# Splitting the weights of a stage's last slab and the next two ahead of the norm, in buffers of their own

## The chip, the cores and the metric

The kernel runs on one core of one Trainium2 chip. The metric is the device time of one execution in microseconds (us), and the number given for a kernel is the median of its timed runs. TensorE (PE) multiplies, VectorE (DVE), ScalarE (ACT) and GpSimd (POOL) do the elementwise work, SyncE (SP) starts transfers. Each engine works through its own instructions in order and waits at semaphores for the others.

## The reference

Two layers of a decoder over x of 512 tokens by 1024 channels, all in float32. A layer runs three token mixers on the same x (a diagonal state-space model "S5", causal pooling, sparse attention), merges them with gates, multiplies by an output matrix, adds the residual and normalizes; then a SwiGLU feed-forward part does the same with its own output matrix and norm. Cut to what matters here:

```python
for l in range(2):
    m = merged(s5(u), pool(u), attention(q, k, v), gates)   # all of them products of x with w_in
    x = layer_norm(alpha * x + m @ w_out, g1, b1)            # norm 0 (layer 0), norm 2 (layer 1)
    h = silu(x @ w_gate) * (x @ w_up)
    x = layer_norm(alpha * x + h @ ffn_w_out, g2, b2)        # norm 1 (layer 0), norm 3 (layer 1)
```

Four norms, then: after three of them the next products need the new x, after the last (norm 3) the output is stored.

## The kernel before

**Products.** Every float32 factor is split in two rounded parts, high and low, and a product is three matmuls: high by high, low by high, high by low. The weights come as a stream of 264 slabs of 128 partitions by 1024 values. SP loads slab n into `raw[n % 2]` as soon as slab n-2 has been split; ACT writes its high part to `whi[n % 2]` (`split_hi`, L973), DVE its low part to `wlo[n % 2]` (`split_lo`, L1373), PE multiplies. ACT's split of slab n waits until PE has finished slab n-2, whose buffer it overwrites: `slab_done` counts finished slabs from 2 up, so "slab n-2 done" is the value n+1.

**An output stage** (`to_tokens`, L587) makes 4 token tiles of 128 by 1024 in PSUM: the first 512 channels with the stage's first half of slabs, the other 512 with the second. Its last slab, b, uses the ordinary buffer `b % 2`. Token tile 3 is finished last, behind the first turning back.

**A norm** works on two halves of the tokens (tiles 0 and 1, tiles 2 and 3). For a half DVE takes statistics from PSUM (L1443), ACT the root (L986), DVE the scalars (L1457, L1459); the normalized tile goes to `xt` by DVE (`first_columns`, L1480, the first 512 channels) and by ACT (`normalized`, L988, the rest); PE turns it back to channels by tokens with 16 transposes (`turn_back`, L575); ACT applies gain and shift in four quarters of 256 channels (`gained`, L997, which raises `ln_x`); DVE splits each quarter into `xh` and `xl` (`halves`, L1461, which raises `x_ready`).

**The first pair of slabs after a norm** (`first_pair`, L616; slabs "at" and "at+1") can start before all of x is there. `x_quarter` (L543) is 6 matmuls of one slab, one token half and one quarter of the channels. In the kernel before the order is: slab at with the first token half, all 4 quarters; `turn_back` of the second half; slab at+1 with the first half; slab at with the second half, at which it counts as done; slab at+1 with the second half. The splits of these two slabs stand in the middle of the norm on ACT (L1015, L1020) and on DVE (L1494, L1509).

**What follows the pair** is slab at+2, in `x_slab` (L537). Its split needs `whi[0]`, and its wait, written once for all slabs, is for slab at done. ACT has one more step ahead of it which waits for the same: it reads slab at's result from PSUM (the tanh in L1357 in the feed-forward part, the copy in L1051 at the start of a layer).

**GpSimd at the start of layer 1** (from L456): it waits for the end of layer 0's last stage, starts two transfers of 2 MB (`w1`, weights of the attention's compression) to SBUF; waits for the whole of the new x and stores it to DRAM in four transfers (`scr_x`); then computes the powers of the state-space model, which it ends with `lam_ready` and, much later, `eph_ready`. DVE waits for the first in `coefficients`, for the second in its first `scan` (L1687). Ahead of each of its waits POOL drains, and it makes the descriptors of its own transfers.

Of the kernel before, what the change touches and what calls it, by code (L numbers as in the profile page):

```python
# [72 lines left out]
def build_program(nc, wstream, w1s, smalls, norms, consts, xin, pos, out):  # L73
# [45 lines left out]
    gates = place("gates", big_at, [P, 16, S])  # L119
    xt = place("xt", xf_at, [P, 4, D])  # L120
# [134 lines left out]
    with ctx:  # L255
# [155 lines left out]
        def _(pool):  # L411
# [44 lines left out]
            for l in range(L):  # L456
# [69 lines left out]
        def _(pe):  # L526
# [16 lines left out]
            def x_quarter(n, half, g, x_before):  # L543
# [4 lines left out]
                for k in (2 * g, 2 * g + 1):  # L548
                    wh, wl = whi[:, n % 2, k * P:k * P + P], wlo[:, n % 2, k * P:k * P + P]
# [14 lines left out]
            def token_products(slot, fh, t, k0, hi, lo, last):  # L564

                dst = ps[:, tile_bank(fh, t), :]
                for q in range(2):
                    a, b = hi[:, k0 + q, P * t:P * t + P], lo[:, k0 + q, P * t:P * t + P]
                    wh, wl = whi[:, slot, S * q:S * q + S], wlo[:, slot, S * q:S * q + S]
# [5 lines left out]
            def turn_back(n, half, rt):  # L575

                if half == 0 or n == 2 * L - 1:
                    pe.wait_ge(ln_first, n + half + 1)
# [8 lines left out]
            def to_tokens(n, at, pairs, hi, lo, freed, taken, each, rt):  # L587

                for fh in range(2):
# [3 lines left out]
                    for s in range(pairs - 2 * fh):  # L593
# [4 lines left out]
                        for t in range(4):  # L598
                            m = token_products(c % 2, fh, t, 2 * s, hi, lo, fh == 0 and s == pairs - 1)
                        m.then_inc(slab_done, 1)  # L600
                a, b = at + 2 * pairs - 2, at + 2 * pairs - 1
                k = 2 * pairs - 4
                pe.wait_ge(lo_ready, a + 3)
                for t in (0, 1):
                    token_products(a % 2, 1, t, k, hi, lo, False)
                pe.wait_ge(lo_ready, b + 3)
                for t in (0, 1):
                    token_products(b % 2, 1, t, k + 2, hi, lo, True).then_inc(t_psum, 1)
                for t in (2, 3):
                    m = token_products(a % 2, 1, t, k, hi, lo, False)  # L610
                m.then_inc(slab_done, 1)
                token_products(b % 2, 1, 2, k + 2, hi, lo, True).then_inc(t_psum, 1)
                turn_back(n, 0, rt)
                token_products(b % 2, 1, 3, k + 2, hi, lo, True).then_inc(slab_done, 1)

            def first_pair(n, at, rt):  # L616

                pe.wait_ge(lo_ready, at + 3)
                for g in range(4):
                    x_quarter(at, 0, g, n * 8)  # L620
                if n:
                    turn_back(n - 1, 1, rt)
                pe.wait_ge(lo_ready, at + 4)
                for g in range(4):
                    x_quarter(at + 1, 0, g, n * 8)
                for c in range(2):
                    for g in range(4):
# [1520 lines left out]
```

## Time and profile before

| what | value |
|---|---|
| time, median of 3 runs | 1764.71 us (1764.57 to 1766.1) |
| the profiled execution, first to last instruction | 1767.2 us |
| PE busy | 1733.0 us, 98% of the span |
| DVE busy | 944.0 us, 53% |
| ACT busy | 649.2 us, 37% |
| POOL busy | 125.6 us, 7% |
| mean clock granted to TensorE | 0.997 of full speed |
| share of PE in the chain that ended last | 86% |

The profile is one execution, which took 2.5 us more than the median of the timed runs. PE is busy nearly everywhere, so what matters are the few places at which it waits, or runs at the lower of its two clocks; the means of the page don't show these. In the rows below a line of the timeline has the start in us, the duration in us, the engine, the line of the kernel, the operation, out<-in, partitions by elements, the count, and in brackets how long the engine had been idle and for whom.

### The profile page before, as it was taken

The page shows a single profiled execution, that of the slowest core. Times are in us where ns is not written, and L with a number is a line of the kernel's source. Part 1 is how long each engine was busy: PE and PEld are TensorE (multiplying, and loading weights), DVE is VectorE, ACT ScalarE, POOL GpSimd, SP SyncE. Part 2 cuts the span into 40 slices and gives each one's busy share as a digit, 9 for nine tenths or more (in the row PEclk, how much of TensorE's full clock was granted, in tenths as well). Part 3 has the DMA queues.
Part 4 walks back from the last instruction along what each step waited for, and adds up shares of the span by engine and source line. Part 5 has one row for each costly group of instructions (what it writes and reads, how often), then busy time and mean ns, then how long its engine had stood idle before and what let it go on. Part 6 is the DMA issues. An engine that isn't in the chain of part 4 may idle for free.

```text
span 1767.2 us, 26801 instructions
## 1 busy us (share of the span) xinstructions
PE 1733.0 (98%) x10172; PEld 1409.5 (80%) x10172; DVE 944.0 (53%) x1514; ACT 649.2 (37%) x1152; POOL 125.6 (7%) x252
## 2 busy tenths in 40 slices
PE   7999999999999999999999999999999999999998
PEld 6778777788888888888888777777888888888886
DVE  5788778444354444422358877775453544444223
ACT  4333666422252222221353346664222522222112
POOL 4700000000000000000037000000000000000000
PEclk9999999999999999999999999999999999999999
DMA  7443111133513222222263431112233222222222
GB/s 259 157 117 88 53 50 49 49 101 102 169 63 105 95 95 95 95 96 95 91 244 110 116 86 50 53 37 72 96 119 119 82 98 95 95 95 95 96 96 83
DMA packets 65918, 174.88 MB, mean 99 GB/s; under 512 B 14256, under 2 KB 26576, under 8 KB 65056
## 3 DMA queue, kind: packets, MB, share of 16 engines
q1 hardware_dynamic: 40192, 140.53, 24.5%
q10 hardware_dynamic: 21888, 13.64, 3.2%
q0 software_dynamic: 3744, 19.41, 3.2%
q8 instruction: 66, 1.08, 0.3%
q14 instruction: 28, 0.23, 0.1%
HBM read 162.27 MB, written 7.08 MB: 96 GB/s over the span
## 4 chain that ended last, share of the span: by engine, by line
PE 86%; DVE 7%; DVEq 3%; ACT 2%; issue 1%; DMA 0%; ACTq 0%
PE ps L532 19%; PE ps L534 18%; PE ps L533 18%; PE ps L572 6%; PE ps L570 6%; PE ps L571 6%; PE ps L857 2%; PE ps L844 2%; PE ps L830 1%; DVE wlo L1376 1%; PE ps L550 1%; PE ps L561 1%; PE ps L552 1%; PE ps L551 1%; PE ps L583 1%
## 5 line engine op out<-in xcount | busy, mean ns | idle before, releaser
L532 PE MATMUL ps<-xh,whi 128*128 128x512 f32 x1312 | 520.0, 396 | 8.4 <-ACT gates L1190 5.1
L534 PE MATMUL ps<-xh,wlo 128*128 128x512 f32 x1312 | 511.3, 390 | 0.0
L533 PE MATMUL ps<-xl,whi 128*128 128x512 f32 x1312 | 510.9, 389 | 0.0
L1376 DVE TENSOR_TENSOR wlo<-raw,whi 128x1024 fp32r<-128x1024 f32 x264 | 324.9, 1231 | 347.4 <-ACT whi L977 338.2
L977 ACT ACTIVATE whi<-raw 128x1024 fp32r<-128x1024 f32 x264 | 278.9, 1057 | 351.0 <-PE ps L572 234.3
L532 PEld LDWEIGHTS ps<-xh,whi 128*128 128x128 f32 x1312 | 246.4, 188 | 61.4 <-issue 7.8
L534 PEld LDWEIGHTS ps<-xh,wlo 128*128 128x128 f32 x1312 | 246.3, 188 | 52.3
L533 PEld LDWEIGHTS ps<-xl,whi 128*128 128x128 f32 x1312 | 246.6, 188 | 48.8 <-issue 0.5
L570 PE MATMUL ps<-whi,hh 128*128 128x512 f32 x352 | 137.5, 391 | 0.0
L572 PE MATMUL ps<-whi,hl 128*128 128x512 f32 x352 | 137.0, 389 | 0.0
L571 PE MATMUL ps<-wlo,hh 128*128 128x512 f32 x352 | 137.0, 389 | 0.0
L1360 ACT ACTIVATE hh<-fb 128x512 f32 (+1 forms) x44 | 27.8, 632 | 201.8 <-DVE fb L1382 201.8
L1382 DVE TENSOR_TENSOR fb<-fa,ps 128x512 f32<-128x512 f32 x44 | 30.2, 687 | 110.9 <-PE ps L534 110.7
L416 POOL TENSOR_TENSOR carry<-carry 1x1 f32<-1x1 f32 x21 | 5.2, 248 | 1176.2 <-PE ps L572 419.5
L1977 DVE SCALAR_TENSOR_TENSOR fa<-ft,ps 128x512 f32<-128x512 f32 x44 | 30.3, 688 | 99.5 <-ACT ft L1357 99.5
L572 PEld LDWEIGHTS ps<-whi,hl 128*128 128x128 f32 x352 | 66.1, 188 | 13.8
L570 PEld LDWEIGHTS ps<-whi,hh 128*128 128x128 f32 x352 | 66.1, 188 | 13.7 <-DVE wlo L1376 0.3
L571 PEld LDWEIGHTS ps<-wlo,hh 128*128 128x128 f32 x352 | 66.1, 188 | 13.6
L1357 ACT ACTIVATE ft<-ps 128x512 f32<-128x512 f32 x44 | 26.3, 598 | 132.7 <-PE ps L534 128.7
L1255 ACT ACTIVATE prob<-ps,tiny 128x128 f32<-128x128 f32 (+3 forms) x128 | 66.3, 525 | 20.4 <-DVE tiny L1802 20.3
L1802 DVE TENSOR_REDUCE tiny<-ps 128x2 f32<-128x256 f32 (+3 forms) x64 | 52.4, 819 | 11.8 <-PE ps L833 11.8
L550 PE MATMUL ps<-xh,whi 128*128 128x256 f32 x128 | 39.5, 309 | 15.7 <-DVE wlo L1376 9.9
(338 smaller groups left out, 2335.5 us busy)
## 6 DMA issues: line engine op xcount, KB each, us to landing
raw<-wstream SPq DMA_DIRECT2D x264, 512.0 KB, 3.3
w<-w1s POOLq DMA_DIRECT2D x4, 2048.0 KB, 11.7
sm<-smalls POOLq DMA_DIRECT2D x2, 1060.0 KB, 6.7
xt<-xin ACTq DMA_DIRECT2D x4, 512.0 KB, 6.3
scratch_u<-pa ACTq DMA_DIRECT2D x8, 256.0 KB
toep<-scratch_k ACTq DMA_DIRECT2D x4, 512.0 KB
toep_b<-scratch_k ACTq DMA_DIRECT2D x4, 512.0 KB
xt<-xin POOLq DMA_DIRECT2D x4, 512.0 KB, 4.0
```

Of the source, the lines that this page charges most:

```text
L532: pe.matmul(ps[:, bank, :], wh, hi[:, k, :], start=first and i == 0, stop=False)
L533: pe.matmul(ps[:, bank, :], wh, lo[:, k, :], start=False, stop=False)
L534: m = pe.matmul(ps[:, bank, :], wl, hi[:, k, :], start=False, stop=last and i == len(blocks) - 1)
L550: pe.matmul(dst, wh, xh[:, k, cols], start=k == 0, stop=False)
L570: pe.matmul(dst, a, wh, start=False, stop=False)
L571: pe.matmul(dst, a, wl, start=False, stop=False)
L572: m = pe.matmul(dst, b, wh, start=False, stop=last and q == 1)
L844: m = pe.transpose(ps[:, bank, at + P * k:at + P * k + P], prob[:, i % 3, kv, P * k:P * k + P], ident)
L977: act.activation(whi[:, c % 2, :], raw[:, c % 2, :], ACT.Copy).then_inc(hi_ready, 1)
L1255: x = act.activation(prob[:, i % 3, kv, 0:n], ps[:, sbank(i) + kv, 0:n], ACT.Exp, bias=tiny[:, 28 + 8 * (i % 3) + kv:29 + 8 * (i % 3) + kv ...
L1376: dve.tensor_tensor(wlo[:, c % 2, :], raw[:, c % 2, :], whi[:, c % 2, :].bitcast(f32), SUB).then_inc(lo_ready, 1)
L1802: dve.tensor_reduce(tiny[:, 28 + 8 * (i % 3):30 + 8 * (i % 3)], ps[:, sbank(i):sbank(i) + 2, 0:n], AX.X, MAX, negate=True).then_inc(s_max, 1)
```

## The change

The last slab b of each output stage and, before norms 0 to 2, the two slabs at and at+1 are split into new buffers, `whi_end` and `wlo_end`, three slots each. These lie where `hh` or `gates` lie, whose first blocks nobody reads any more by then. The splits of all three now wait for slab b-3 done and stand ahead of the norm on ACT and on DVE (`stage_splits`, `split_end_hi`, `split_end_lo`); no split is left in the norm.

`first_pair` takes its quarters in turn through both slabs: quarters 0 and 1 of at, 0 and 1 of at+1, then 2 and 3 alternately; then the turning back; then each quarter of the second token half for at and for at+1. Slab at therefore counts as done 6 matmuls ahead of slab at+1, where before it was 24. The very first pair of the kernel keeps its old order (`first_slabs`). The split of slab at+2 and its wait are unchanged.

In the norm DVE takes the second quarter ahead of the last tile's statistics, and the normalized first 512 channels of tile 3 stay with DVE while those of tile 2 stay with ACT, so that ACT has three such steps instead of four. POOL stores x first, then waits for slab at+1 done (since `w1` lies over the new buffers) and then loads `w1`. The diff, cut:

```diff
+    whi_end = place("whi_end", big_at, [P, 3, 1024], f32r)
+    wlo_end = place("wlo_end", big_at + 3072, [P, 3, 1024], f32r)
...
                 if l:
-                    wait(slab_done, l * NSLAB + 2)
-                    load_w1()
-
-                if l:
                     wait(ln_x, l * 16)
                     for t in range(4):
                         pool.dma_start(scr_x[:, t, :], xt[:, t, :]).then_inc(x_stored, 16)
+                    wait(slab_done, l * NSLAB + 4)
+                    load_w1()
...
             def first_pair(n, at, rt):
 
+                pe.wait_ge(lo_ready, at + 4)
+                for c, g in ((0, 0), (0, 1), (1, 0), (1, 1), (0, 2), (1, 2), (0, 3), (1, 3)):
+                    x_quarter(at + c, 0, g, n * 8)
+                turn_back(n - 1, 1, rt)
+                for g in range(4):
+                    for c in range(2):
                         m = x_quarter(at + c, 1, g, n * 8)
-                    m.then_inc(slab_done, 1)
+                        if g == 3:
+                            m.then_inc(slab_done, 1)
...
+            def split_end_hi(c, slot, free):
+
+                act.wait_ge(raw_loaded[c % 2], (c // 2 + 1) * 16)
+                act.wait_ge(slab_done, free + 3)
+                act.activation(whi_end[:, slot, :], raw[:, c % 2, :], ACT.Copy).then_inc(hi_ready, 1)
+
+            def stage_splits(at, pairs, last):
+
+                b = at + 2 * pairs - 1
+                split_end_hi(b, 0, b - 3)
+                if not last:
+                    split_end_hi(b + 1, 1, b - 3)
+                    split_end_hi(b + 2, 2, b - 3)
...
-                    for fh in (0, 1) if half and n < 2 * L - 1 else (1,):
+                    for fh in (0, 1) if t == 2 and n < 2 * L - 1 else (1,):
...
                 first_columns(0)
                 second_stats(n, 2, next_slab + 2)
-                if not last:
-                    split_lo(0, next_slab)
                 halves(n, 0, 0, rt, last)
-                if last:
-                    halves(n, 0, 1, rt, last)
+                halves(n, 0, 1, rt, last)
                 second_stats(n, 3, next_slab + 2)
                 variances(1)
...
-                    halves(n, 0, 1, rt, last)
+                    halves(n, 0, 2, rt, last)
                     scalars(n, 1)
-                    for g in (2, 3):
-                        halves(n, 0, g, rt, last)
-                    split_lo(0, next_slab + 1)
+                    halves(n, 0, 3, rt, last)
+                    first_columns(1)
```

What stands in a row on DVE in norm 0 of the kernel before, from the statistics of tile 2 to the end of the first token half (`wlo` is a split of weights, CAST and the TENSOR_TENSOR to `xl` are one quarter of x):

```order
L1443 BN_STATS lnst<-ps 128x6 [waits t_psum]
L1445 BN_AGGR lnmv<-lnst 128x2
L1376 TENSOR_TENSOR wlo<-raw,whi 128x1024 [waits hi_ready]
L1474 CAST xh<-xt 128x2x256 [waits ln_x]
L1382 TENSOR_TENSOR xl<-xt,xh 128x2x256
L1443 BN_STATS lnst<-ps 128x6 [waits slab_done]
L1445 BN_AGGR lnmv<-lnst 128x2
L1451 TENSOR_SCALAR lnrs<-lnmv 128x2
L1474 CAST xh<-xt 128x2x256 [waits ln_x]
L1382 TENSOR_TENSOR xl<-xt,xh 128x2x256
L1457 RECIPROCAL lnrs<-lnrs 128x2 [waits ln_sd]
L1459 SCALAR_TENSOR_TENSOR lnnb<-lnmv,lnrs 128x2
```

And of the changed kernel, from the same statistics on (`L1477` and `L1479` are the statistics there):

```order
L1477 BN_STATS lnst<-ps 128x6 [waits t_psum]
L1479 BN_AGGR lnmv<-lnst 128x2
L1508 CAST xh<-xt 128x2x256 [waits ln_x]
L1416 TENSOR_TENSOR xl<-xt,xh 128x2x256
L1508 CAST xh<-xt 128x2x256 [waits ln_x]
L1416 TENSOR_TENSOR xl<-xt,xh 128x2x256
L1477 BN_STATS lnst<-ps 128x6 [waits slab_done]
L1479 BN_AGGR lnmv<-lnst 128x2
L1485 TENSOR_SCALAR lnrs<-lnmv 128x2
L1508 CAST xh<-xt 128x2x256 [waits ln_x]
L1416 TENSOR_TENSOR xl<-xt,xh 128x2x256
L1491 RECIPROCAL lnrs<-lnrs 128x2 [waits ln_sd]
```

The split of the weights is gone from this stretch and the second quarter has moved ahead of the last tile's statistics.

On POOL at the start of layer 1, before (`w` is `w1`, the memsets of `php` begin the powers):

```order
L416 TENSOR_TENSOR carry<-carry 1x1 [waits slab_done]
L465 DMA w_58<-w1s 128x4096 x2
L416 TENSOR_TENSOR carry<-carry 1x1 [waits ln_x]
L474 DMA scratch_x<-xt 128x1024 x4
L416 TENSOR_TENSOR carry<-carry 1x1 [waits sincos_ready]
L477 MEMSET php 128x16
```

And of the changed kernel:

```order
L418 TENSOR_TENSOR carry<-carry 1x1 [waits ln_x]
L472 DMA scratch_x<-xt 128x1024 x4
L418 TENSOR_TENSOR carry<-carry 1x1 [waits slab_done]
L467 DMA w_60<-w1s 128x4096 x2
L418 TENSOR_TENSOR carry<-carry 1x1 [waits sincos_ready]
L477 MEMSET php 128x16
```

The store of x and the load of `w1` have changed places, and the wait between them is now for finished slabs.

## Rows read from the trace of the kernel before

**Rows 1.** Timeline of PE, norm 0: turning back, last tile, first pair.
```profile
507.90 0.49 PE L583 MATMUL ps<-cn,xt 128*128 128x128 f32 x3
...
510.80 0.40 PE L572 MATMUL ps<-whi,mgl 128*128 128x512 f32 x1
511.75 0.36 PE L550 MATMUL ps<-xh,whi 128*128 128x256 f32 x1 [0.56 <-DVE xl L1382]
...
513.89 0.39 PE L550 MATMUL ps<-xh,whi 128*128 128x256 f32 x1 [1.19 <-DVE xl L1382]
...
517.86 0.49 PE L583 MATMUL ps<-cn,xt 128*128 128x128 f32 x3
519.52 0.36 PE L550 MATMUL ps<-xh,whi 128*128 128x256 f32 x1
```

**Rows 2.** Timeline of DVE and ACT in norm 0.
```profile
508.54 3.75 ACT L1006 ACTIVATE xt<-ps,nrm 128x256 f32<-128x256 f32 x8 [0.20 <-PE ps L583]
...
509.27 1.23 DVE L1376 TENSOR_TENSOR wlo<-raw,whi 128x1024 fp32r<-128x1024 f32 x1 [0.19 <-issue]
...
510.91 0.69 DVE L1382 TENSOR_TENSOR xl<-xt,xh 128x512 fp32r<-128x512 f32 x1
...
513.14 0.69 DVE L1382 TENSOR_TENSOR xl<-xt,xh 128x512 fp32r<-128x512 f32 x1
...
514.18 2.78 ACT L993 ACTIVATE xt<-ps,lnnb,lnrs 128x512 f32<-128x512 f32 x4 [0.26 <-DVE lnnb L1459]
...
514.55 0.69 DVE L1382 TENSOR_TENSOR xl<-xt,xh 128x512 fp32r<-128x512 f32 x1
...
520.04 0.69 DVE L1382 TENSOR_TENSOR xl<-xt,xh 128x512 fp32r<-128x512 f32 x1
...
521.15 0.69 DVE L1382 TENSOR_TENSOR xl<-xt,xh 128x512 fp32r<-128x512 f32 x1
```

**Rows 3.** Windows: length, busy (instructions) of PE, PEld, DVE, ACT, POOL; clock, DMA, GB/s.
```profile
96.00:97.00 1.00, 1.00 (x5) 0.81 (x6) 1.00 (x2) 0.00 (x0) 0.00 (x0) 1.00 0.52 76
515.00:516.00 1.00, 1.00 (x5) 0.70 (x5) 0.93 (x3) 1.00 (x2) 0.00 (x0) 0.50 0.00 0
```

**Rows 4.** Timeline behind the first pair after norm 0, four engines.
```profile
525.24 0.28 PE L552 MATMUL ps<-xh,wlo 128*128 128x256 f32 x1
...
525.56 0.60 ACT L1357 ACTIVATE ft<-ps 128x512 f32<-128x512 f32 x1 [2.02 <-PE ps L552]
...
527.13 1.22 DVE L1376 TENSOR_TENSOR wlo<-raw,whi 128x1024 fp32r<-128x1024 f32 x1 [0.26 <-ACT whi L977]
...
528.41 0.50 PE L532 MATMUL ps<-xh,whi 128*128 128x512 f32 x1
```

**Rows 5.** Timeline of PE: the same two ends at norms 1 and 2.
```profile
878.96 0.49 PE L583 MATMUL ps<-cn,xt 128*128 128x128 f32 x3
...
899.75 0.50 PE L532 MATMUL ps<-xh,whi 128*128 128x512 f32 x1
...
1383.00 1.58 PE L583 MATMUL ps<-cn,xt 128*128 128x128 f32 x13
...
1402.59 0.50 PE L532 MATMUL ps<-xh,whi 128*128 128x512 f32 x1
```

**Rows 6.** Timeline of PE in layer 0: the longest wait inside the stages.
```profile
95.90 0.50 PE L532 MATMUL ps<-xh,whi 128*128 128x512 f32 x1 [1.95 <-DVE wlo L1376]
```

**Rows 7.** Timeline of POOL, PE and DVE at the start of layer 1.
```profile
882.46 0.57 POOL L465 DMA_DIRECT2D w<-w1s  x1
...
910.75 0.18 POOL L416 TENSOR_TENSOR carry<-carry 1x1 f32<-1x1 f32 x1 [8.90 <-issue]
...
964.96 0.13 POOL L506 MEMSET r8m<- 128x16 f32 x1
...
970.59 0.50 PE L532 MATMUL ps<-xh,whi 128*128 128x512 f32 x1 [0.75 <-DVE wlo L1376]
...
977.28 0.42 DVE L1382 TENSOR_TENSOR sct<-eph,ps 128x256 f32<-128x256 f32 x1 [0.16 <-issue]
```

More of the change, by code:

```diff
@@ L562, in residual, with token_products @@
                                   start=m == 0, stop=False, is_transpose=True)
-            def token_products(slot, fh, t, k0, hi, lo, last):
+            def token_products(high, low, fh, t, k0, hi, lo, last):
                 dst = ps[:, tile_bank(fh, t), :]
@@ L1018, in ln_part @@
                 deviations(n, 1)
-                if not last:
-                    split_hi(0, next_slab + 1)
                 normalized(n, 1, rt)
@@ L1344, in _ @@
                         merged_hi(c // 5 - 1)
-                for c in range(1, NO):
+                for c in range(1, NO - 1):
                     split_hi(0, l * NSLAB + OO + c)
@@ L1348, in _ @@
                         merged_hi(3)
+                stage_splits(l * NSLAB + OO, KD // 2, False)
                 ln_part(l * 2, l * NSLAB + OF, xt)
@@ L1365, in _ @@
                     ff_pairs(hl_ + OF // 2 + 2 + i * 2, i + 1, False)
-                for c in range(1, NG):
+                for c in range(1, NG - 1):
                     split_hi(0, l * NSLAB + OG + c)
+                stage_splits(l * NSLAB + OG, KF // 2, l == L - 1)
                 ln_part(l * 2 + 1, (l + 1) * NSLAB, xt)
@@ L1480, in first_columns @@
                 def first_columns(half):
-                    for t in (2 * half, 2 * half + 1):
+                    for t in (2 * half, 2 * half + 1) if half == 0 or last else (3,):
                         x = dve.tensor_scalar(rt[:, t, 0:S], ps[:, tile_bank(0, t), :], lnmv[:, t, 0:1], lnrs[:, t:t + 1], SUB, MUL)
@@ L1492, in ln_part @@
                 second_stats(n, 2, next_slab + 2)
-                if not last:
-                    split_lo(0, next_slab)
                 halves(n, 0, 0, rt, last)
-                if last:
-                    halves(n, 0, 1, rt, last)
+                halves(n, 0, 1, rt, last)
                 second_stats(n, 3, next_slab + 2)
@@ L1957, in _, with stage @@
                         x.then_inc(mg_raw, 1)
-                def stage(at, pairs, last_low=False):
-                    for c in range(1, 2 * pairs):
+                def stage(at, pairs, last_low=False, last=False):
+                    b = at + 2 * pairs - 1
+                    for c in range(1, 2 * pairs - 1):
                         if c == pairs + 1:
@@ L1965, in stage @@
                             low_parts(3)
+                    split_end_lo(b, 0)
+                    if not last:
+                        split_end_lo(b + 1, 1)
+                        split_end_lo(b + 2, 2)
                 stage(l * NSLAB + OO, KD // 2, True)
@@ L1991, in _ @@
                     ff_pairs(hl_ + OF // 2 + 2 + i * 2, i + 1, False)
-                stage(l * NSLAB + OG, KF // 2)
+                stage(l * NSLAB + OG, KF // 2, last=l == L - 1)
                 ln_part(l * 2 + 1, (l + 1) * NSLAB, xt)
```

48 lines of the change are left out of this document (29 added, 19 removed).

## The prediction

> **What bounds the kernel now.** I read the page first: PE is busy 98% of the span, so only its waits and its slow stretches can be gained. The waits of PE send me to the three norms that are followed by products, and the timeline of PE there gives the shape. I count from t0, the first transpose of the first turning back (507.90 in norm 0). PE starts its last matmul of token tile 3 at 510.80, is free 0.23 us later, at t0+3.1, waits 0.56 us for the first quarter of x and 1.19 us for the second [rows 1]. The reason is DVE: a split of weights of 1.23 us at 509.27 stands ahead of the first quarter, whose low part only starts at 510.91, and the statistics of tile 3 stand between it and the second quarter, which starts at 513.14 [rows 2]. The windows show a second loss: in 515 to 516 PE is busy all the time, but at a granted clock of 0.50, the lower level of 1.2 GHz [rows 3]. At the other end, slab at+2 starts at 528.41 [rows 4], t0+20.5. The same stretch takes 899.75 - 878.96 = 20.8 us at norm 1 and 1402.59 - 1383.00 = 19.6 us at norm 2 [rows 5]. I take 19.6 us as its length at full clock, and the 0.9 and 1.2 us more as the price of the slow clock in norms 0 and 1.
>
> **The change, part by part.**
>
> *The first token half.* ACT starts the gains at t0+0.64 and needs 3.75 / 4 = 0.94 us for a quarter [rows 2]. Without the split, DVE starts when the first quarter lands. The second token half shows how long that is: turning back starts at 517.86 [rows 1], the low part of its first quarter starts at 520.04 and takes 0.69 [rows 2], 2.87 us in all. So the first quarter is there at t0+2.9, before PE is free at t0+3.1: the wait of 0.56 goes. The second quarter follows 1.1 us later (520.04 to 521.15), at t0+4.0. The third stands behind the statistics; the distance 510.91 to 513.14, 2.2 us, puts it at t0+6.2. The fourth comes 1.4 us behind it (513.14 to 514.55, scalars included), at t0+7.6 [rows 2]. PE: a quarter of one slab is 6 matmuls; between the first behind the turning back at 519.52 [rows 1] and the last of slab at at 525.24 [rows 4] lie 47 steps, 0.122 us each, so 0.73 us for a quarter. It takes quarter 0 of at (to 3.9), then quarter 1 and both of at+1 (4.0 to 6.2), both third quarters (to 7.7), both fourth (to 9.2). All four waits are covered by the other slab. The second turning back needs ACT as well: three steps of the four that take 2.78 [rows 2], 2.1 us, from about t0+6.6, is t0+8.7, earlier. It starts at t0+9.2.
>
> *The second token half.* In the kernel before, slab at+1's first half, 24 matmuls, stood behind this turning back and covered the 2.87 us until the next quarter of x. Now nothing stands there. The transposes take 519.52 - 517.86 = 1.66 us [rows 1], to t0+10.9; the quarter is there at t0+12.1: a new wait of 1.2 us. From there PE needs 1.46 us for a quarter of both slabs and DVE delivers one every 1.1, so 48 matmuls run through, to t0+17.9. So far the change is ahead by 1.5 us: in norm 2 the pair ended 0.2 us before slab at+2 started, at 19.4.
>
> *What is late next: the split of slab at+2.* ACT must wait for slab at done, read its result from PSUM, then split; DVE then makes the low part. In the kernel before: last matmul of at 525.24, ACT 525.56, DVE 527.13 for 1.22, PE 528.41, 3.17 us, hidden behind the 24 matmuls of at+1 [rows 4]. The queue is the same in the changed kernel, but at is now done only 6 matmuls ahead of at+1. The last matmul of at starts at 12.1 + 41 x 0.122 = t0+17.1; plus 3.17 is t0+20.2. PE is free at t0+17.9 and waits 2.3 us. On ACT the reading and the split stand behind that wait, DVE's split behind ACT, everything of slab at+2 behind both. At norm 1 the copy of L1051 takes the place of the tanh, with the same length.
>
> *Sum of a norm at full clock:* 20.2 against 19.6, so 0.6 us worse, three times: +1.8 us. Against what the profiled execution took (20.5, 20.8, 19.6) it is 60.6 - 60.9 = -0.3 us.
>
> *The clock.* In norm 0 the waits of 0.56 and 1.19 us brought the slow clock [rows 1, 3]; by the lengths norm 1 had it too and norm 2 had not; in layer 0 one wait of 1.95 us [rows 6] did not bring it either, 96 to 97 ran at 1.00 [rows 3]. The changed norm has 1.2 us and, 6 us later, 2.3 us in one piece, longer than any of those. I give each norm a chance of 0.65. The price is bounded below by what it cost before, 0.9 us, where part of it hid behind waits for x, and above by a stretch like 514 to 517.6, 3.6 us at half speed, 1.8 us; behind the pair PE has no waits for tens of us, so I take the upper end. Two of three: +3.6 us.
>
> *The splits ahead of the norm.* The same number of instructions, moved to before the first statistics, where ACT and DVE wait for PE. No gain and no loss: PE's matmuls of slab b followed without a gap before. If the loads came late, DVE's 1.23 us splits would push the statistics; I bound that at 0 to 0.7 us a norm and take 0. Norm 3 and the first pair of the kernel keep their order: 0.
>
> *POOL in layer 1.* Its store and its load, issue and descriptors together, took from 882.46 to 910.75, 28.3 us, a good part of it before x was whole [rows 7]. Now both lie behind it. The last gain of norm 1 ends at 878.96 + 9.2 + 0.6 + 3.75 = 892.5, so the powers begin near 920 to 921 instead of 911, 9 to 10 us later, and `eph_ready` moves from 965 to about 974.5. DVE reads these values at 977.28 [rows 7]: still in time, by under 3 us. A gain is possible too: in 943 to 970 DVE worked beside POOL's largest instructions and PE waited 0.75 us at the end of it [rows 7]; with POOL later that can vanish, no more. Bounds -0.75 and +4, taken: -0.3, near the lower one because the margin holds.
>
> As to this, the Trainium skill (GPSIMD Engine Reference, section 8, Key points) says that GpSimd shares its SBUF interfaces with VectorE and contends with DVE instructions of two SBUF inputs. DVE's part of this stretch is mostly such instructions; by that rule the contention moves with POOL and the sum would stay within the same bounds.
>
> **Sum.** The profiled execution: 1767.2 - 0.3 + 3.6 - 0.3 = 1770.2. It lies 2.5 us over the median of the timed runs, about what its two slow stretches cost (0.9 + 1.2), so I take the typical timed run to have full clock in the norms: 1764.7 + 1.8 + 3.6 - 0.3 = 1769.8; allowing for a slow stretch in some runs of before, 1769.5.
>
> **The rivals.** A measurement can tell about 0.2%, 3.5 us, from no change; so faster is under 1761.2 and slower over 1768.2.
>
> 1. *The clock holds or falls once.* Everything as above, but the gap leaves the clock mostly alone: 1764.7 + 1.5 = 1766.2, or 1768 with one. For it: norm 2 and the wait of 1.95. Against it: norms 0 and 1 fell with less in one piece. Chance 0.30. The Trainium skill (TensorE: Matmul & The Clock Gate, HAM oscillation) would have only idle gaps clearly longer than these re-throttle the array; by that rule this rival is the outcome, but this trace shows the lower level after gaps of 0.56 and 1.19 us, so the rows decide against giving it more.
>
> 2. *The handover does not cost* because the reading and the split overlap with the end of at+1 more than I see, or the second half runs ahead: then the pair's gain stands, 17.9 + 0.2 against 19.6, -1.5 x 3 = -4.5, and with -0.3 it is 1760. Nothing in the rows shortens the 3.17 us. Chance 0.05.
>
> 3. *POOL comes too late.* If descriptors or contention stretch its chain by more than 3 us, DVE's scan waits, and PE, which needs the scan's result some 6 us later, waits with it: +1 to +4 on top, 1773. Chance 0.10, from a drift of 3 in a chain of 55 us.
>
> 4. *All three norms fall:* 1771.3. Chance 0.15. The forecast with two has 0.40.
>
> **How the numbers follow.** The predicted time is that of the forecast, 1769.5. Slower: forecast 0.40, all three 0.15, POOL 0.08 of its 0.10, makes 0.63. Same: the first rival 0.30 and 0.02 of the third, 0.32. Faster: 0.05. The range takes in the clock holding everywhere with the small bounds below it (1765.5) and POOL's case (1773.5).
>
> **What would show it.** In the profile of the changed kernel: no wait for x of over 0.3 us in the first token half; the second turning back at t0+9.2; then PE waiting 1.2 us for `xl`; then 2.3 us at the first matmul of slab at+2 with the split of the weights on DVE as releaser, three times; half clock in the first us of that slab. On POOL the powers near 920, DVE's scan without a wait. I am wrong if slab at+2 starts within 0.5 us of the pair's end, if the turning back comes later than t0+10, or if PE waits anew between 970 and 990.

## The result and the profile after

The changed kernel takes 1774.46 us (median of 4 runs, 1771.99 to 1775.45), the kernel before 1764.64 us in the same comparison. The ratio is 1.0048, 95% interval [1.0035, 1.006]: slower, by some 8.5 us. A second comparison, below, gives 1.0036 [1.0022, 1.0049]. The profiled execution of the changed kernel has a span of 1772.0 us from first to last instruction and took 1773.82, so the rows below are those of a typical run.

In every run that has both numbers the time is 1.7 to 1.9 us longer than the span. The 1767.2 us of the profile before are a span, so that execution took some 1769 us. It lay about 4.3 us over the median and not 2.5, which matters for the prediction's view of the clock.

The waits of PE, summed over the whole profile of the changed kernel, name the places at once (columns: total us, times, longest):

```profile
PE ps L532 <- DVE wlo L1405: 11.7, 6, 3.0
...
PE ps L553 <- DVE xl L1416: 3.1, 3, 1.0
```

The first row is the first matmul of a slab waiting for the low part of its weights; the second is the first quarter of x behind the second turning back. In norm 0 the timeline of PE in the changed kernel reads as follows (start, length, line, operands, and in brackets the idle time before and what ended it); [rows 1, 4] are what it answers to.

```profile
507.48 1.91 PE L585 MATMUL ps<-cn,xt 128*128 128x128 f32 x16
...
516.71 1.91 PE L585 MATMUL ps<-cn,xt 128*128 128x128 f32 x16
519.64 0.39 PE L553 MATMUL ps<-xh,whi_end 128*128 128x256 f32 x1 [1.03 <-DVE xl L1416]
...
527.84 0.50 PE L532 MATMUL ps<-xh,whi 128*128 128x512 f32 x1 [2.18 <-DVE wlo L1405]
```

Between 510.4 and 516.7 nothing stands idle any more: the waits of 0.56 and 1.19 us of [rows 1] are gone. In their place stand 1.03 and 2.18 us. ACT and DVE show why the second one is there (same kernel, same place):

```profile
524.98 0.60 ACT L1385 ACTIVATE ft<-ps 128x512 f32<-128x512 f32 x1 [2.58 <-PE ps L555]
525.48 1.05 ACT L994 ACTIVATE whi<-raw 128x1024 fp32r<-128x1024 f32 x1
...
526.56 1.23 DVE L1405 TENSOR_TENSOR wlo<-raw,whi 128x1024 fp32r<-128x1024 f32 x1 [0.26 <-ACT whi L994]
```

ACT waits 2.58 us for slab at, reads its result, makes the high part, DVE makes the low part, and only then can slab at+2 begin. It is the same chain as in [rows 4], but the matmuls of slab at+1 no longer stand behind it. At the other two norms the same two starts read:

```profile
880.50 1.94 PE L585 MATMUL ps<-cn,xt 128*128 128x128 f32 x16 [0.38 <-ACT xt L1024]
...
900.91 0.50 PE L532 MATMUL ps<-xh,whi 128*128 128x512 f32 x1 [2.17 <-DVE wlo L1405]
...
1387.08 1.91 PE L585 MATMUL ps<-cn,xt 128*128 128x128 f32 x16
...
1407.45 0.50 PE L532 MATMUL ps<-xh,whi 128*128 128x512 f32 x1 [2.17 <-DVE wlo L1405]
```

The clock behind the wait of 2.2 us, in windows of 1 us behind norm 0, norm 1 and norm 2 (columns as in [rows 3]; the third number from the end is the granted clock):

```profile
530.00:531.00 1.00, 1.00 (x4) 0.80 (x3) 0.85 (x2) 0.18 (x1) 0.00 (x0) 0.50 0.62 246
902.00:903.00 1.00, 1.00 (x4) 0.75 (x3) 0.30 (x2) 1.00 (x1) 0.56 (x2) 0.50 0.97 328
...
1408.00:1409.00 1.00, 1.00 (x6) 0.80 (x5) 0.30 (x2) 0.79 (x2) 0.00 (x0) 1.00 0.51 115
```

It fell to the level of 1.2 GHz behind norms 0 and 1 and stayed at 2.4 GHz behind norm 2.

The largest single loss lies elsewhere, in layer 1 (timeline of PE; before it was 0.75 us at 970.59 [rows 7]):

```profile
975.59 0.50 PE L532 MATMUL ps<-xh,whi 128*128 128x512 f32 x1 [2.98 <-DVE wlo L1405]
```

The windows behind that wait show the lower clock once more:

```profile
977.00:978.00 1.00, 1.00 (x4) 0.81 (x3) 0.85 (x3) 0.00 (x0) 0.00 (x0) 0.50 1.18 220
```

DVE ahead of it, in the changed kernel, and POOL beside it:

```profile
962.10 0.43 DVE L1416 TENSOR_TENSOR hgt<-hid 128x256 f32<-128x256 f32 x1
...
964.44 1.37 DVE L1416 TENSOR_TENSOR ta<-lam,bch 128x512 f32<-128x512 f32 x1
965.73 1.53 DVE L1416 TENSOR_TENSOR tb<-lam,bch 128x512 f32<-128x512 f32 x1
...
971.96 1.60 DVE L1416 TENSOR_TENSOR vmat_b<-ta,tb 128x512 f32<-128x512 f32 x1
973.49 2.05 DVE L1405 TENSOR_TENSOR wlo<-raw,whi 128x1024 fp32r<-128x1024 f32 x1
```

```profile
964.22 2.50 POOL L444 TENSOR_TENSOR r8m<-eph,st 128x512 f32<-128x512 f32 x2
...
971.48 1.54 POOL L444 TENSOR_TENSOR eph<-r8m 128x512 f32<-128x512 f32 x1
973.14 1.31 POOL L504 COPY r8m<-rp 128x1024 f32<-128x1024 f32 x1
974.58 0.12 POOL L506 MEMSET r8m<- 128x16 f32 x1
```

and the same DVE instructions in the kernel before, where POOL's last large step had ended at 964.96 [rows 7]:

```profile
965.21 0.69 DVE L1382 TENSOR_TENSOR ta<-lam,bch 128x512 f32<-128x512 f32 x1
...
968.71 0.69 DVE L1382 TENSOR_TENSOR vmat_b<-ta,tb 128x512 f32<-128x512 f32 x1
969.32 1.22 DVE L1376 TENSOR_TENSOR wlo<-raw,whi 128x1024 fp32r<-128x1024 f32 x1
```

Six instructions of 0.69 us took 1.37 to 1.63 us each beside POOL's, and the split behind them 2.05 instead of 1.22. From the first of them to the end of the split it is 11.1 us instead of 5.3, so 5.8 us more. DVE had come to them 3.5 us earlier in the stage (its start moved from 965.21 to 964.44, while PE's program stood 2.8 us later by then), so 2.2 us of it came out as idle time of PE, and the slow stretch came on top.

To add up, I use the first transpose of each first turning back, t0, as a milestone. It cuts the program into three stretches: A from norm 0 to norm 1, B from norm 1 to norm 2 with the stages of layer 1, C from norm 2 to norm 3. C holds one norm and no POOL work, and in most kernels no slow stretch either. "Falls" counts the slow stretches of the clock behind norms 0, 1 and 2; the one in 977 to 978 is not among them and lies in B.

| profiled execution | A | B | C | falls |
|---|---|---|---|---|
| before | 371.06 | 504.04 | 370.13 | 2 |
| changed | 373.02 | 506.58 | 370.88 | 2 |
| changed, second profile | 372.82 | 506.55 | 370.86 | 2 |

Changed against before is +2.0, +2.5 and +0.75 us; t0 of norm 0 itself came 0.4 us earlier, so the span is 4.8 us longer. The medians differ by more (9.8 us in the first comparison, 6.8 in the second). The profiled execution of before is one with two slow stretches, as the prediction said.

### The profile page after: what moved, and what is told of

Same layout as the page of the kernel before. It is cut to its first block, busy times and chain, and to the rows that moved or that the text cites. A ratio compares the mean times of both kernels' runs of the same rounds, so it can differ in the third digit from the quotient of the medians.

```text
span 1772.0 us, 26801 instructions
## 1 busy us (share of the span) xinstructions
PE 1735.2 (98%) x10172; PEld 1413.0 (80%) x10172; DVE 944.8 (53%) x1517; ACT 647.1 (37%) x1149; POOL 125.6 (7%) x252
## 3 DMA queue, kind: packets, MB, share of 16 engines
q8 instruction: 66, 1.08, 0.3%
## 4 chain that ended last, share of the span: by engine, by line
PE 87%; DVE 6%; ACT 3%; DVEq 2%; issue 1%; DMA 1%; ACTq 0%; SPq 0%
PE ps L532 19%; PE ps L534 18%; PE ps L533 18%; PE ps L573 6%; PE ps L574 6%; PE ps L575 6%; PE ps L874 2%; PE ps L861 2%; PE ps L847 1%; PE ps L553 1%; DVE wlo L1405 1%; PE ps L554 1%; PE ps L555 1%; PE ps L690 1%; PE ps L564 1%
## 5 line engine op out<-in xcount | busy, mean ns | idle before, releaser
L1405 DVE TENSOR_TENSOR wlo<-raw,whi 128x1024 fp32r<-128x1024 f32 x254 | 312.9, 1232 | 336.2 <-ACT whi L994 327.2
L994 ACT ACTIVATE whi<-raw 128x1024 fp32r<-128x1024 f32 x254 | 268.4, 1057 | 333.3 <-PE ps L575 216.7
L573 PE MATMUL ps<-whi,hh 128*128 128x512 f32 x336 | 131.2, 391 | 0.0
L575 PE MATMUL ps<-whi,hl 128*128 128x512 f32 x336 | 130.9, 390 | 0.0
L574 PE MATMUL ps<-wlo,hh 128*128 128x512 f32 x336 | 130.9, 390 | 0.0
L874 PEld LDWEIGHTS ps<-probt,vtok 128*64 128x64 f32 x640 | 33.6, 136 | 23.0 <-issue 23.0
```

The lines of the kernel that those rows point to most:

```text
L573: pe.matmul(dst, a, wh, start=False, stop=False)
L574: pe.matmul(dst, a, wl, start=False, stop=False)
L575: m = pe.matmul(dst, b, wh, start=False, stop=last and q == 1)
L874: pe.matmul(ps[64 * kv:64 * kv + 64, 7, P * t:P * t + P], vtok[:, br, k, 64 * kv:64 * kv + 64], probt[:, i % 2, kv, P * k:P * k + P], star ...
L994: act.activation(whi[:, c % 2, :], raw[:, c % 2, :], ACT.Copy).then_inc(hi_ready, 1)
L1405: dve.tensor_tensor(wlo[:, c % 2, :], raw[:, c % 2, :], whi[:, c % 2, :].bitcast(f32), SUB).then_inc(lo_ready, 1)
```

## The experiments

The theory after the comparison: three things move the time. The quarters remove waits (gain), slab at+2 waits for the handover (loss), and POOL's exchanged order puts its large steps beside DVE instructions that PE is waiting for (loss). Rivals: the exchanged order costs because its results or `w1` come too late; or the 3 us wait is an accident of one execution. Kernels that are compared in one table below shared their runs of before.

**POOL's order taken back, all else changed.** The two end slabs of norm 1 move into buffers of their own, so that `w1` can be loaded where it was.

```diff
+    whi_alt = place("whi_alt", ys_at, [P, 2, 1024], f32r)
+    wlo_alt = place("wlo_alt", ys_at + 2048, [P, 2, 1024], f32r)
...
                 if l:
+                    wait(slab_done, l * NSLAB + 2)
+                    load_w1()
                     wait(ln_x, l * 16)
                     for t in range(4):
                         pool.dma_start(scr_x[:, t, :], xt[:, t, :]).then_inc(x_stored, 16)
-                    wait(slab_done, l * NSLAB + 4)
-                    load_w1()
```

> The changed kernel with one part undone: POOL again loads w1 first and stores x behind it, as in the kernel before (to allow it, the two slabs after norm 1 are split into a place that w1 does not cover). Theory A (POOL's later chain of powers works beside DVE's longest instructions and delays the split that PE waits for near 975 us): that wait falls from 2.98 us back to under 1 us, no slow clock follows it, and the kernel is 3 to 4 us faster than the changed one, about 6 us (0.34%) slower than the kernel before. Rival B (all of the loss is the handover at the norms): no change against the changed kernel, ratio 1.005, and a wait of about 3 us stays near 975 us.

**POOL's order alone, in the kernel before.** The same four lines the other way round, nothing else.

> The kernel before with only POOL's order changed: x is stored first, w1 loaded after slab at+1. Theory A: the powers start 9 us later, PE waits about 3 us instead of 0.75 near 971 us, a stretch at the lower clock may follow; 2 to 4 us slower than the kernel before (0.11 to 0.23%). Rival B: within 1 us of the kernel before.

**Alternating alone, in the kernel before.**

```diff
-                for c in range(2):
-                    for g in range(4):
-                        m = x_quarter(at + c, 1, g, n * 8)
-                    m.then_inc(slab_done, 1)
+                for i in range(8):
+                    c, g = (i % 2, i // 2) if n else (i // 4, i % 4)
+                    m = x_quarter(at + c, 1, g, n * 8)
+                    if g == 3:
+                        m.then_inc(slab_done, 1)
```

> The kernel before with only one thing changed: behind norms 0 to 2 the second token half of the first pair goes quarter by quarter through both slabs, so that slab at is done 6 matmuls ahead of slab at+1 instead of 24. Theory H (the split of slab at+2 waits for slab at done): PE waits 2.2 us behind each of the three pairs, in some followed by the lower clock (1.8 us each); slower by 6.6 to 12 us (0.37 to 0.68%). Rival (the handover's chain overlaps with the pair and costs little): within 2 us of the kernel before.

**The handover taken away from the changed kernel.** ACT and DVE split slab at+2 right behind the norm, when the last quarter of x has been made, and not after slab at.

```diff
+            def split_next_hi(at):
+                act.wait_ge(raw_loaded[0], (at // 2 + 2) * 16)
+                act.wait_ge(slab_done, at + 1)
+                act.activation(whi[:, 0, :], raw[:, 0, :], ACT.Copy).then_inc(hi_ready, 1)
...
+                split_next_hi(l * NSLAB + OF)
...
+                split_lo(0, l * NSLAB + OF + 2)
```

> The changed kernel with one addition: slab at+2 is split right behind the norm on ACT and DVE, without waiting for slab at done, since its buffer is free by then. Theory H: the waits of 2.2 us behind the three pairs vanish and with them the lower clock there; the kernel gains 6.6 us and 1.8 us for each slow stretch of the changed one, 8 to 11 us, and ends within 2 us of the kernel before, with the loss near 975 us left. Rival (the lower clock comes from the wait of 1.0 us behind the second turning back, or from elsewhere): slow stretches stay and the gain is 6 us at most.

Measured, all four beside the same 22 runs of before (median 1767.66 us):

| kernel | median us | ratio | A | B | C | falls |
|---|---|---|---|---|---|---|
| changed, POOL as before | 1769.76 | 1.0014 [1.0005, 1.0023] | 371.15 | 503.15 | 370.89 | 1 |
| before, POOL exchanged | 1773.20 | 1.0031 [1.0018, 1.0043] | 371.75 | 506.61 | 370.13 | 1 |
| before, alternating | 1776.01 | 1.0045 [1.0031, 1.0059] | 374.13 | 504.38 | 375.02 | 5 |
| changed, early split | 1769.69 | 1.0007 [0.9998, 1.0016] | 368.72 | 510.24 | 368.41 | 0 |

POOL's order is a cost of its own. Added to the kernel before it makes 5.5 us; taken out of the changed one, stretch B falls from 506.55 to 503.15, by 3.4 us, while C stays at 370.9, and no wait of over 0.3 us is left near 975. Two expectations were off in size. The changed kernel with POOL as before was to stay about 6 us over the kernel before and stays 2.1 over it; the early split was to gain 8 to 11 us on the changed kernel and gains 5 to 7 by the ratios. In the kernel with the exchanged order alone PE stands still for the same reason as in the changed one, at the next split in the row (first fence PE, second DVE):

```profile
980.49 0.76 PE L530 MATMUL ps<-xh,whi 128*128 128x512 f32 x1 [4.22 <-issue]
```

```profile
973.69 1.45 DVE L1380 TENSOR_TENSOR ta<-lam,sm 128x576 f32<-128x576 f32 x1
...
976.74 1.67 DVE L1393 SCALAR_TENSOR_TENSOR wmat_b<-ta,tb 128x576 f32<-128x576 f32 x1
978.33 2.05 DVE L1374 TENSOR_TENSOR wlo<-raw,whi 128x1024 fp32r<-128x1024 f32 x1
```

The profile puts this wait down to "issue", but the split on DVE ends at 978.33 + 2.05 = 980.38 and PE starts 0.11 us later. So when the profile names no releaser, it is worth a look at the other engines.

The alternation alone shows the handover in its pure form: it adds a wait of 2.18 us ahead of slab at+2 to the waits that the kernel before has anyway (PE, norm 2):

```profile
1392.80 0.39 PE L550 MATMUL ps<-xh,whi 128*128 128x256 f32 x1 [1.24 <-DVE xl L1383]
1394.21 0.58 PE L550 MATMUL ps<-xh,whi 128*128 128x256 f32 x1 [0.44 <-DVE xl L1383]
1409.96 0.50 PE L532 MATMUL ps<-xh,whi 128*128 128x512 f32 x1 [2.18 <-DVE wlo L1377]
```

Here the clock fell twice at norm 1 and twice at norm 2, and once behind norm 0. C is 4.9 us longer than in before. With the early split instead, A and C are the shortest of the table, 368.4 for C against 370.88 of the changed kernel: 2.5 us a norm, the 2.2 us of the handover and a little more. Its B is the longest, though (510.24): two waits of 2.68 and 4.22 us stand there, at 929.33 and 979.91, with POOL's order still the exchanged one. The second is the contention again. The first is not: the DVE instructions ahead of it take 0.68 to 0.78 us. There ACT's split was late, since its slab had not landed (ACT, early split):

```profile
917.62 1.06 ACT L994 ACTIVATE whi<-raw 128x1024 fp32r<-128x1024 f32 x1 [5.72 <-DMA raw<-wstream]
```

POOL issued `w1`, 4 MB, at 899.70 here, 18 us ahead of that split; in the kernels with POOL's order of before it is issued near 882 to 884. That the load held the slab back is likely, but not shown by itself. If both waits are the work of POOL's order, they must go with it; the next group tests that.

**Contention or lateness?** The kernel before, with POOL kept busy beside DVE and with nothing moved:

```diff
                 pool.memset(r8m[:, :, 0:1], 0.0).then_inc(eph_ready, 1)
+                if l:
+                    for i in range(6):
+                        tt(spare[:, :], sin_t[:, 0:448], cos_t[:, 0:448], MUL)
+                        pool.drain()
```

> The kernel before, with six more POOL products of 128x448 f32 (each followed by a drain, into 448 elements of free space, from the two rotation tables) right behind the memset of r8m that releases eph_ready in layer 1. POOL's powers, its loads and every wait stand where they stood, so nothing of POOL's comes later that anyone needs before 980 us; what is new is only that POOL works from about 965.1 to 974 beside DVE. Theory 1 (contention: DVE's operations with two SBUF inputs take about twice as long beside POOL's): the six 512-element operations of DVE at 965.2 to 969.3 take 1.4 to 1.6 us each, not 0.69, and the low split behind them 2.0, not 1.22, so the split that PE waits for at 970.59 comes 4 to 5 us later, PE stands idle 4 to 6 us in place of 0.75, the granted clock falls to 0.5 for some 3 us behind it, and the time rises by 5 to 8 us, as with the order of POOL alone (+5.5). Theory 2 (lateness: the exchanged order costs because w1, the powers or eph_ready come later): DVE's rows unchanged, time within 1 us of before.

**Slab by slab instead of alternating**, in the changed kernel with POOL's order of before:

```diff
-                for g in range(4):
-                    for c in range(2):
-                        m = x_quarter(at + c, 1, g, n * 8)
-                        if g == 3:
-                            m.then_inc(slab_done, 1)
+                for c in range(2):
+                    for g in range(4):
+                        m = x_quarter(at + c, 1, g, n * 8)
+                    m.then_inc(slab_done, 1)
```

> The changed kernel with POOL's order of before, and with the second token half slab by slab (four quarters of slab at, then four of at+1) in place of alternating. Nothing is left out of the computation. With the alternation this kernel took 1769.76 us beside 1767.66 of before (+2.1). Theory 1 (the alternation's handover costs: the split of slab at+2 waits for slab at, 6 matmuls ahead in place of 24): the 2.17 us idle piece at slab at+2 goes at norms 1 to 3; in its place each quarter of slab at waits about 0.4 us for its xl (DVE hands over a quarter each 1.1 us, PE uses it in 0.7), some 1.0 to 1.3 us per norm, so some 1 us per norm and the clock's fall are saved: 1766 to 1768, -2 to -4 us against the alternating one. Theory 2 (alternating hides as much as it costs): within 1 us of 1769.8.

**Both costs taken out**: early split and POOL's order of before, together in the changed kernel.

> The changed kernel with both suspected costs taken out: slab at+2 is split right behind the norm, without waiting for slab at (so the 2.2 us handover cannot arise), and POOL loads w1 ahead of its powers, as in the kernel before (the two next slabs of norm 1 then lie in buffers at ys_at, outside w1). Nothing is left out of the computation. Theory (handover and POOL's place are the two costs, the rest of the change gains): the kernel with early splits alone stood at +2.0 us against before (1769.69 to 1767.66) and the order of POOL alone at +5.5 (1773.2 to 1767.66), so 2.0 - 5.5 = -3.5 us: about 1764, ratio 0.998; no PE idle piece over 0.3 us at slab at+2 of any norm, none near 976 to 981, only the 1.0 us wait for xl behind the second turning back; granted clock full behind the norms. Rival (the gains of the quarters are worth nothing, the early splits only move the cost): within 0.1% of before, 1766 to 1769.

**The changed kernel again**, beside the same runs of before:

> The changed kernel itself, for its ratio on the same chip as the other three and a second profile. From the first measurement 1.0048 [1.0035, 1.006]; with before near 1767.7 on this chip some 1776. If POOL's place (+5.5 alone, -6.3 when taken back) and the handover explain it: idle pieces of 2.2 us at slab at+2 of the three norms and of about 3 us near 975.6, the latter in every profile. Rival (the 3 us piece belongs to one execution): gone here.

Measured, beside 19 runs of before (median 1766.79 us):

| kernel | median us | ratio | A | B | C | falls |
|---|---|---|---|---|---|---|
| before, POOL busy | 1773.02 | 1.0031 [1.0021, 1.0041] | 371.57 | 507.97 | 370.13 | 2 |
| changed, POOL as before, slab by slab | 1765.75 | 0.9992 [0.9983, 1.0001] | 370.31 | 503.33 | 369.88 | 0 |
| changed, early split, POOL as before | 1760.10 | 0.9960 [0.9946, 0.9974] | 368.93 | 499.32 | 368.40 | 0 |
| changed | 1773.60 | 1.0036 [1.0022, 1.0049] | 372.82 | 506.55 | 370.86 | 2 |

For the wait near 976 it is contention, not lateness: six products that nobody waits for cost 6.2 us by the medians, with the same ratio of 1.0031 as the exchanged order, and stretch B alone is 3.9 us longer. Its rows differ from what I had expected in the place: POOL was done with its powers at 962, so the products ran from there. POOL, then DVE, then PE:

```profile
962.02 8.70 POOL L443 TENSOR_TENSOR spare<-sin_t,cos_t 128x448 f32<-128x448 f32 x6
```

```profile
962.38 2.15 DVE L1381 TENSOR_TENSOR wlo<-raw,whi 128x1024 fp32r<-128x1024 f32 x1
964.45 1.37 DVE L1387 TENSOR_TENSOR hgt<-hid 128x256 f32<-128x256 f32 x1
965.90 1.08 DVE L1721 TENSOR_SCALAR hgt<-hgt 128x256 f32<-128x256 f32 x1
...
969.81 1.47 DVE L1387 TENSOR_TENSOR ta<-lam,bch 128x512 f32<-128x512 f32 x1
971.20 0.68 DVE L1387 TENSOR_TENSOR tb<-lam,bch 128x512 f32<-128x512 f32 x1
```

```profile
975.97 0.51 PE L537 MATMUL ps<-xh,whi 128*128 128x512 f32 x1 [3.84 <-DVE wlo L1381]
```

The same instruction `hgt<-hid` takes 0.43 us in the changed kernel at 962.10, where POOL was at small steps, and 1.37 here. With POOL's last product over at 970.72, DVE is back at 0.68 us for 512 elements. Of the six steps that were expected to suffer only the first did (1.47 us), but those ahead of them did, and the end is the same: the split that PE needs is late. PE also waits 1.14 us at 964.63, 0.1 us behind the end of the split of 2.15 us.

Slab by slab gives back 3.9 us against the alternating kernel (ratios 1.0014 and 0.9992, 0.22% of 1767), and 1.0 us of stretch C, as the first theory had it: the idle piece ahead of slab at+2 is gone at every norm, the clock did not fall, and the waits of the quarters that take its place are all under 0.3 us each. With both costs out the two waits of 2.68 and 4.22 us are gone (0.34 us is left at 966.96), B is 499.32, and the kernel beats before: 1760.10 us, 0.9960. That is more than the 0.998 that was expected from adding the two effects. They don't simply add: with the early split the exchanged order costs 10.9 us of B (510.24 against 499.32), with the handover in place 3.4. The two waits make 6.9 us of the first, and the clock is low beside them, in 930 to 934 and in 978 to 985.

**One quarter behind the second turning back.** In the fastest version the wait for `xl` of 1.03 us is left. One quarter moves behind the turning back to cover it, and the fastest version runs again beside it.

```diff
-                for c, g in ((0, 0), (0, 1), (1, 0), (1, 1), (0, 2), (1, 2), (0, 3), (1, 3)):
+                for c, g in ((0, 0), (0, 1), (1, 0), (1, 1), (0, 2), (1, 2), (0, 3)):
                     x_quarter(at + c, 0, g, n * 8)
                 turn_back(n - 1, 1, rt)
+                x_quarter(at + 1, 0, 3, n * 8)
```

> The fastest version so far (early splits, POOL's order of before; 1760.1 us beside 1766.79 of before on its chip), with one quarter of the first token half moved behind the second turning back, to cover its 1.03 us wait for xl. The turning back then starts some 0.5 us earlier (it waits some 0.2 us for the normalized values), and a quarter takes 0.7: of the 1.03 us some 0.5 stay. Theory (what PE waits for there sets the time): 0.5 us less at each of three norms, 1.5 in all, so 0.9950 to 0.9955 of before, beside 0.996. Rival (ACT's and DVE's chain behind the second turning back sets the end of the pair, so that order on PE matters only where it moves that start): the wait behind it shrinks by 0.7 but 0.2 to 0.5 comes back ahead of the turning back, under 0.5 us in all, not to be told from 0.996.

> The fastest version so far once more, as the thing to compare the moved quarter with on the same chip, and to see whether its ratio to before, 0.996 [0.9946, 0.9974] on the other chip, stands. Theory (POOL's place and the handover were the two costs, the quarters gain): again 0.995 to 0.997. Rival (the 3 us beyond the 3.5 that were expected there belonged to that chip): 0.998.

Measured beside 10 runs of before (median 1766.56 us): 1759.33 us, 0.9959 [0.9945, 0.9972], and for the fastest version again 1760.64 us, 0.9966 [0.9954, 0.9978]. The timeline of PE in the kernel with the moved quarter:

```profile
517.15 1.94 PE L596 MATMUL ps<-cn,xt 128*128 128x128 f32 x16
518.85 0.36 PE L564 MATMUL ps<-xh,whi_end 128*128 128x256 f32 x1
...
520.12 0.39 PE L564 MATMUL ps<-xh,whi_end 128*128 128x256 f32 x1 [0.33 <-DVE xl L1438]
```

The wait shrinks from 1.03 to 0.33 us. Some 0.3 us comes back ahead of the turning back: with one quarter of 0.73 us less in front of it, it should start at t0+8.5, and does at 517.15 - 508.32 = t0+8.83. Stretch C, 368.39 to 368.04, gains 0.35 us, which three times makes 1 us: halfway between the two expectations (1.5 and under 0.5), and less than the medians (1.3 us apart, intervals overlapping) can tell. A is 0.7 us shorter too, but B is 1.2 us longer (501.01 against 499.78), with waits of 0.70 and 1.34 us in layer 1. That the fastest version beats before is shown twice; that the quarter adds to it is not.

## Why the prediction was right, and where it was not

The forecast was slower, at 1769.5 us with a range to 1773.5. It is slower, at 1774.46: the sign is right, the size is 5 us short. The time lies 1 us over the range; by the ratio, 1764.7 x 1.0048 = 1773.2, it lies just inside.

Part of this is luck. The prediction took 3.5 us for the least difference that can be told, and with POOL's order of before its norms and its clock come to 1.0014 [1.0005, 1.0023], +2.5 us by the ratio (2.1 by the medians). So the part that was argued for does not make the kernel slower by that measure. The term that does is POOL's, which stood at -0.3.

- **The first token half: right.** No wait is left, and the second turning back starts at 516.71 - 507.48 = t0+9.23; the prediction said t0+9.2.
- **The new wait for `xl`: right.** The first quarter starts 519.64 - 516.71 = 2.93 us behind the turning back, for 2.87 predicted. The wait itself is 1.03 us and not 1.2, because the 16 transposes keep PE busy for 1.91 us and not only for the 1.66 taken from [rows 1].
- **The handover: right.** Slab at+2 starts at t0+20.36, 20.41 and 20.37 in the three norms, behind 2.17 to 2.18 us of idle time; predicted were t0+20.2 and 2.3 us. Alternating alone brings it, the early split takes it away, slab by slab too. At full clock it was to cost 0.6 us a norm; stretch C shows 370.88 - 370.13 = 0.75.
- **The clock: right for the changed kernel, wrong as a difference.** Two of three norms fell, in both profiles. The price can be read from two kernels that are alike in stretch A but for the fall, the changed one (373.02, 372.82) and the one with POOL's order of before (371.15): 1.7 to 1.9 us, predicted 1.8. But the term of +3.6 took the kernel before to have full clock in its norms, since its profiled execution lay 2.5 us over the median, "about what its two slow stretches cost". It lay some 4.3 over, as said above, and the two stretches are each short of 1.7 us of full clock. The kernels with the norms of before that were profiled later fall there as well (one of three and two of three). Timed runs have a mean granted clock each, too, and one fall lowers it by 1.7 / 1770, about 0.001. Averaged, it is 0.9970 for before (19 runs) and 0.9952 for the changed kernel beside it (5 runs). As an estimate from these two that is 1.8 falls or 3.1 us a run. The stretch at 977 takes 1.7 of it, which leaves 1.4 for the norms if the rest of the kernel falls as often in both. With POOL's order of before the mean is 0.9971 (11 runs) against 0.9965 for before (22 runs): there the changed norms fall no more often than the old ones. These means don't say where a run fell, so how the remainder divides over the norms stays open.
- **POOL: the step that failed.** The term was -0.3 us with bounds of -0.75 and +4. Its timing came true almost to the row: the powers began at 919.74 (predicted 920 to 921), `eph_ready` was given at 974.58 (974.5), the scan's chain did not wait. Its price did not. The prediction asked only whether DVE would wait for POOL's results. It did not ask which DVE instructions POOL's large steps would now lie beside: those right ahead of a split that PE waits for, where the slack was already below zero (0.75 us of waiting, [rows 7]). It had also read the contention in the kernel before as lasting to 970, though POOL's last large step ends at 964.96 [rows 7] and the six DVE steps behind it ran at 0.69 us. The runs give it 3.4 us by stretch B of the profiles and 5.5 us [3.2, 7.6] by the times of the order alone. The third rival had the size, +1 to +4, but the wrong mechanism, a late scan, and no more than 0.10. The prediction also wrote that contention in 943 to 970 could vanish with POOL later. It did vanish there: `hgt<-hid` fell from 1.27 us in the kernel before (the row below) to 0.43. The gain was real, 3.5 us on DVE, and was outweighed by 5.8 us lost right behind.

```profile
960.04 1.27 DVE L1382 TENSOR_TENSOR hgt<-hid 128x256 f32<-128x256 f32 x1
```

On this the Trainium skill (GPSIMD Engine Reference, section 8, Key points) was the sentence to weigh more: GpSimd shares its SBUF interfaces with VectorE and contends with DVE instructions that have two SBUF inputs or run in a 2-port performance mode. The prediction cited it and concluded that "the contention moves with POOL" within the same bounds. The traces agree with the rule and add the size: a factor of 2.0 to 2.4 on two-input instructions of 512 f32 elements. An instruction with one input slowed as well: `hgt<-hgt`, line 1721, took 1.08 us beside POOL and 0.29 (line 1746 of the changed kernel, at 962.61) without. Whether it ran in a 2-port mode no profile here says.

With the terms as measured, the sum is 3 x 0.75 for the handover, 1.4 for the clock in the norms and 3.4 for POOL (its slow stretch included), 7.1 us. The second comparison, from which the clock term is estimated, has +6.4 us by its ratio and +6.8 by its medians. Taking both falls at 1.9 us instead, against a kernel before without any, gives 1764.7 + 2.25 + 3.8 + 3.4 = 1774.1, close to the first median of 1774.46; but the measured clocks don't bear out a kernel before without falls.

The second rival, a handover that doesn't cost, had been priced at -1.5 us a norm. The early split builds it: stretch C is 370.13 - 368.40 = 1.7 us shorter than before's.

## What to carry to other kernels

When a change hands an engine a buffer earlier, look at what freed that buffer in the old order. Two slabs that alternate finish together, and whoever splits the next one waits for both; start that split where its buffer is really free. When work of GpSimd moves in time, ask not only who waits for its results but which VectorE instructions it will lie beside, and whether one of those is the last to be ready for TensorE. Make the moved part a kernel of its own: here one gain (the quarters with an early split, 0.996) had been hidden by two costs of which one had nothing to do with the idea. And before the price of a slow stretch goes into a sum, look whether the old kernel pays it too: the mean clock of its timed runs tells.

## What the runs showed of the hardware

- POOL's instructions of 448 to 512 f32 elements a partition about double the time of DVE's beside them: 1.37 to 1.63 us in place of 0.69 for 512 elements, 2.05 to 2.15 in place of 1.22 for the split of 1024. With POOL kept busy until 970.72 the next DVE instruction, at 971.20, was back at 0.68.
- The clock of PE is not a function of one idle piece. It fell behind the waits of 2.17 to 2.18 us in norms 0 and 1 and not behind the one of 2.17 us in norm 2, in both profiles of the changed kernel; with POOL's order of before, which changes nothing in norm 0, it held in norm 0 as well:

```profile
530.00:531.00 1.00, 1.00 (x6) 0.82 (x5) 0.69 (x1) 1.00 (x2) 0.00 (x0) 1.00 0.86 287
901.00:902.00 1.00, 1.00 (x4) 0.72 (x3) 0.43 (x2) 0.99 (x2) 0.00 (x0) 0.50 0.99 283
```

- The same holds for the wait in layer 0 that [rows 6] show. It stands in all twelve profiles. The clock fell behind it in eight (waits of 1.89 to 2.71 us) and held in four (1.95 to 1.99 us); in the changed kernel it fell in the first profile and held in the second, both times behind 1.98 us. So one execution in which such a wait did no harm, as the prediction's 1.95 us, says little. The first profile of the changed kernel, where the profile before has 1.00:

```profile
96.00:97.00 1.00, 1.00 (x3) 0.78 (x3) 1.00 (x2) 0.00 (x0) 0.00 (x0) 0.50 0.41 109
```

- A stretch at 1.2 GHz behind such a wait costs 1.7 to 1.9 us, nearly as much as the wait itself. So removing a wait of 2.2 us can be worth almost twice its length.
